# Moving the norm's reciprocal root behind the projections in a two-layer encoder

## The reference

```python
def _rms(x, g):
    y = x * rsqrt(mean(x * x, axis=-1) + EPS);  return y * g
# one layer
h = _rms(x, attn_norm);  z = h @ w_in            # 1024 -> 1984 columns
dq, dk = _rope(z[:, :512]), _rope(z[:, 512:1024])
dv, c_q, c_kv, k_pe = z[:, 1024:1536], z[:, 1536:1792], z[:, 1792:1920], z[:, 1920:]
y_diff = _rms(differential_attention(dq, dk, dv), diff_subln) * (1 - lam_init)
qh  = _rms(c_q, q_a_norm) @ w_q_b                # 4 heads of 128 + 64 (rope)
kvh = _rms(c_kv, kv_a_norm) @ w_kv_b             # 4 heads of 128 + 128
y_mla = latent_attention(qh, kvh, _rope(k_pe))
x = x + concat(y_diff, y_mla) @ w_o
h = _rms(x, ffn_norm)
x = x + (silu(h @ w_gate) * (h @ w_up)) @ w_down # 1024 -> 2816 -> 1024
```

## Time and profile before

| | |
|---|---|
| median of 3 runs | 2709.67 us |
| the profiled execution: its own time, its span | 2709.78 us, 2707.8 us |
| mean granted TensorE clock | 0.967 |
| TensorE busy | 2484.6 us (92%), 11236 matmuls |
| VectorE busy | 1328.9 us (49%) |
| ScalarE busy | 569.0 us (21%) |
| GpSimd busy | 892.0 us (33%) |
| the chain that ended last | TensorE 81%, VectorE 14%, issue 3%, ScalarE 1%, DMA 1% |

### The profile page before, as it was taken

One profiled execution on the slowest core, in us unless ns is written; L12 is line 12 of the kernel. 1 busy time (PEld: TensorE's weight loads), 2 busy tenths in 40 slices (PEclk: granted clock), 3 DMA queues, 4 the chain that ended last, 5 costly groups with the idle time before them and its releaser, 6 DMA issues.

```text
span 2707.8 us, 30377 instructions
## 1 busy us (share of the span) xinstructions
PE 2484.6 (92%) x11236; PEld 2024.4 (75%) x11236; DVE 1328.9 (49%) x2312; ACT 569.0 (21%) x1089; POOL 892.0 (33%) x434
## 2 busy tenths in 40 slices
PE   4888899896999999999989889988799999999996
PEld 3666687675888888888867668766578888888885
DVE  4887658857333223322248864886742222222225
ACT  2233314432010101010024341434111101000101
POOL 5431400014666655555210010001434433344421
PEclk9998999898999999999989999999899999999998
DMA  6431342122333333331122224222211111111101
GB/s 236 166 117 47 125 187 94 47 94 94 117 117 122 126 130 125 116 116 70 70 78 109 78 78 156 109 78 79 101 31 51 50 53 47 46 46 46 53 17 62
DMA packets 50339, 249.46 MB, mean 92 GB/s; under 512 B 5968, under 2 KB 6096, under 8 KB 32720
## 3 DMA queue, kind: packets, MB, share of 16 engines
q1 hardware_dynamic: 49824, 245.76, 25.5%
q10 hardware_dynamic: 432, 2.62, 0.2%
HBM read 187.54 MB, written 60.82 MB: 92 GB/s over the span
## 4 chain that ended last, share of the span: by engine, by line
PE 81%; DVE 14%; issue 3%; ACT 1%; DMA 1%; POOL 0%; SPq 0%; DVEq 0%; ACTq 0%; POOLq 0%
PE bank L412 26%; PE bank L413 25%; PE bank L414 25%; PE bank L747 1%; DVE acc L1129 1%; DVE mx L1263 1%; PE bank L614 1%; DVE qpe L1160 1%; DVE aT_lo L1271 1%; PE bank L621 1%; DVE h_lo L1116 1%; DVE h_t L1110 1%; ACT aT_hi L948 1%; DVE ms L1068 1%; DMA w<-parked 1%
## 5 line engine op out<-in xcount | busy, mean ns | idle before, releaser
L412 PE MATMUL bank<-h_hi,w 128*128 128x512 f32 x1792 | 708.8, 396 | 8.5 <-DVE h_lo L1116 6.2
L413 PE MATMUL bank<-h_lo,w 128*128 128x512 f32 x1792 | 701.5, 391 | 0.0
L414 PE MATMUL bank<-h_hi,w 128*128 128x512 f32 x1792 | 701.5, 391 | 0.0
L531 POOL TENSOR_TENSOR w<-raw,zero 128x1024 fp32r<-128x1024 f32 x159 | 314.0, 1975 | 951.7 <-PE bank L414 842.6
L1300 DVE TENSOR_TENSOR gated<-bank,silu 128x512 f32<-128x512 f32 x88 | 60.8, 691 | 749.8 <-PE bank L414 747.0
L412 PEld LDWEIGHTS bank<-h_hi,w 128*128 128x128 f32 x1792 | 339.5, 189 | 91.1 <-DVE h_lo L1116 13.4
L534 POOL TENSOR_TENSOR w<-raw,w 128x1024 fp32r<-128x1024 f32 x159 | 394.8, 2483 | 12.5
L413 PEld LDWEIGHTS bank<-h_lo,w 128*128 128x128 f32 x1792 | 339.3, 189 | 70.9 <-issue 1.7
L414 PEld LDWEIGHTS bank<-h_hi,w 128*128 128x128 f32 x1792 | 338.8, 189 | 71.6
L1310 DVE TENSOR_TENSOR x<-x,bank 128x512 f32<-128x512 f32 x352 | 238.4, 685 | 192.1 <-PE bank L414 191.8
L412 PE MATMUL bank<-u_hi,w 128*128 128x512 f32 x704 | 273.9, 389 | 0.0
(11 more groups left out here) (154 smaller groups left out, 3420.5 us busy)
## 6 DMA issues: line engine op xcount, KB each, us to landing
w<-parked SPq DMA_DIRECT2D x81, 1024.0 KB, 4.8
raw<-in_wffn SPq DMA_DIRECT2D x132, 512.0 KB, 3.6
parked<-w SPq DMA_DIRECT2D x27, 1024.0 KB, 4.8
parked<-p SPq DMA_DIRECT2D x27, 1024.0 KB, 4.9
raw<-in_watt SPq DMA_DIRECT2D x27, 512.0 KB, 5.7
praw<-in_watt SPq DMA_DIRECT2D x27, 512.0 KB, 5.8
out_yT<-y_out SPq DMA_DIRECT2D x16, 256.0 KB, 2.2
x<-in_xT SPq DMA_DIRECT2D x4, 512.0 KB, 5.7
```

Source lines behind the costliest of these rows:

```text
L412: nc.tensor.matmul(out_ap, lhs[0], rhs[0], start=first, stop=False)
L413: nc.tensor.matmul(out_ap, lhs[0], rhs[1], start=False, stop=False)
L414: return nc.tensor.matmul(out_ap, lhs[1], rhs[0], start=False, stop=last)
L531: nc.gpsimd.tensor_tensor(w[slot][0][:], src, zeros_like(src), ALU.add).then_inc(s_hi.sem, 1)
```

## The change

Projections now read x * gain, without the root; the root multiplies their results.

- **x_hi, x_lo**: ACT writes hi = x * gain (scale of the activation), DVE lo = x * gain - hi in one instruction with two SBUF inputs, as soon as a tile of x is there. h_t, AN and the applies are gone.
- **Where the root goes**: into the value projection's evictions (`scale=rstd`, one number per token and partition), into cos and sin tables for the rope tiles (`scaled`), into gate and up of the FFN (DVE multiplies the PSUM tiles in place), and for the latent tiles c_q and c_kv nowhere: their own norm follows, and only its EPS is scaled (`eps_var`).
- **first, next**: sums and spread of the norm are issued behind `values` and ahead of tile k0. ACT's v_hi waits for the root. At the seam of the layers x_lo follows each x add.
- **last**: sums come after both projections of ev 0, the spread after gate of ev 1; DVE adds a square and forms an x_lo in turn.
- **start**: DVE adds the first norm's squares in POOL's place; constants and rope tables are loaded from ACT's queue, x before and between the raw weights.
- **splits**: each of POOL's passes goes in two halves of 512 columns, and RAW is 2.
- **end**: the squares of batch 1 are added between the last x adds; both roots come before the 16 outputs.

```diff
-RAW = 3
+RAW = 2
 # POOL, split and prep
-                nc.gpsimd.tensor_tensor(w[slot][0][:], src, zeros_like(src), ALU.add).then_inc(s_hi.sem, 1)
+                for n, cols in enumerate(spans(2)):
+                    last = nc.gpsimd.tensor_tensor(w[slot][0][:, cols], src[:, cols], zeros_like(src[:, cols]), ALU.add)
+                last.then_inc(s_hi.sem, 1)
 # PE, FFN step 0
-                            if first and tt == 0:
-                                if b == 0:
-                                    pe.wait_ge(s_t_lo.sem, s_t_lo.half_at(l, 1, NSQ - 1))
-                                elif part == 0:
-                                    norm_spread("last", l)
...
-                            if first and ev == 0 and part == 0:
+                            if first and ev == 0 and part == 1:
                                 norm_sums("last", l)
+                            if first and ev == 1 and part == 0:
+                                norm_spread("last", l)
 # PE, halves
-            norm_sums("first", 0)
-            norm_spread("first", 0)
...
+                        if b == 0 and step == ("P", "k0"):
+                            norm_spread("first", l)
                         if kind == "V":
                             values(l, b)
+                            if b == 0:
+                                norm_sums("first", l)
 # ACT
+                nc.scalar.activation(hi[:, k, :], source(which, b, k), ACT.Copy, scale=gain_at(which, l, b, k)).then_inc(
+                    s_x_hi.sem, 1)
...
+                                act.wait_ge(s_dg.sem, s_dg.layer_at(l, 0))
...
-                                nc.scalar.activation(v[0][:, m, :], bank[2 + m][:], ACT.Copy).then_inc(s_plain_hi.sem, 1)
+                                nc.scalar.activation(v[0][:, m, :], bank[2 + m][:], ACT.Copy,
+                                                     scale=rstd[:, m:m + 1]).then_inc(s_plain_hi.sem, 1)
 # DVE
+                nc.vector.scalar_tensor_tensor(lo[:, k, :], source(which, b, k), gain_at(which, l, b, k),
+                                               hi[:, k, :].bitcast(F32), ALU.mult, ALU.subtract).then_inc(s_x_lo.sem, 1)
...
+            for k in range(KT):
+                x_lo("first", 0, 0, k)
+                square_add("first", 0, k)
...
+            def norm_use(which, l, b):
+                dve.wait_ge(s_rb.sem, f(s_rb, st0))
+                if which == "last" or which == "tail" and b == 1:
+                    nc.vector.tensor_copy(scaled[:, half, :], bank[tail][:]).then_inc(s_t.sem, 1)
                 else:
+                    nc.vector.tensor_tensor(scaled[:, 0, :], cs[:, 0, :], bank[tail][:], ALU.mult)
+                    nc.vector.tensor_tensor(scaled[:, 1, :], cs[:, 1, :], bank[tail][:], ALU.mult).then_inc(s_t.sem, 1)
...
                 for k in range(KT):
-                    last_add(l, k)
+                    square_add("last", l, k)
+                    x_lo("last", l, 0, k)
...
+                        nc.vector.tensor_tensor(zg[:], zg[:], scaled[:, b, :], ALU.mult).then_inc(s_gate.sem, 1)
+                        nc.vector.tensor_tensor(zu[:], zu[:], scaled[:, b, :], ALU.mult).then_inc(s_up.sem, 1)
...
+                        nc.vector.tensor_tensor(zu[:], zu[:], silu[ev % 2][:], ALU.mult).then_inc(s_gated.sem, 1)
```

More of the change, by code:

```diff
@@ L143 @@
 NSTAT_LAYER = B * NSTAT + 2
+USED = {}
+NORMED = {}
+for _s in STATS:
+    _n = 2 if _s == "cq" else 1
+    _at = sum(len(v) for v in USED.values())
+    USED[_s] = list(range(_at, _at + _n))
+    if _s != "n":
+        _at = sum(len(v) for v in NORMED.values())
+        NORMED[_s] = list(range(_at, _at + _n))
+NUSED = sum(len(v) for v in USED.values())
+NUSED_LAYER = B * NUSED + 2
+NNORMED = sum(len(v) for v in NORMED.values())
+NSPLIT_LAYER = (B + 2) * KT
 NEV = 2 * 16 + 16
@@ L1055, in _, with rsqrt_diagonal @@
             assert pre[0] == PRE_DVE
-            def rsqrt_diagonal(link, width, src, wait, done, dg=dg):
+            def rsqrt_diagonal(link, width, src, wait, done, dg=dg, eps=None, keep=False):
                 dve.wait_ge(*wait)
@@ L1311, in _, with down_add @@
-                link, n = chain(lambda j: s_link.layer_at(l, s_link.layer + j))
-                norm_rsqrt("next", l, 0, link)
+                def down_add(c, ev):
+                    dve.wait_ge(s_mm.sem, s_mm.step_at(l, c, 8 + ev))
+                    dve.wait_ge(s_xf.sem, s_xf.step_at(l, c, ev - 2 * KT))
+                    xn = x[:, ev // KT, ev % KT, :]
+                    nc.vector.tensor_tensor(xn, xn, bank[4 + ev % 4][:], ALU.add).then_inc(s_xf.sem, 1)
+                with dve.Fori(0, FC - 1) as c:
+                    gated_step(c)
+                    for ev in range(B * KT):
+                        down_add(c, ev)
@@ L1314, in _ @@
+                gated_step(FC - 1)
+                for ev in range(KT):
+                    down_add(FC - 1, ev)
+                link, n = chain(lambda j: s_link.layer_at(l, s_link.layer + j))
+                if l < L - 1:
+                    for k in range(KT):
+                        down_add(FC - 1, KT + k)
+                        x_lo("next", l, 0, k)
+                    norm_rsqrt("next", l, 0, link)
             n = [0]
@@ L1342, in _ @@
             assert n[0] == FINAL_DG
-            for m in range(4, B * KT):
-                if m == KT:
-                    dve.wait_ge(s_pe, 2)
+            dve.wait_ge(s_rb.sem, s_rb.layer_at(L, 0))
+            for m in range(KT):
+                output(m)
+            dve.wait_ge(s_pe, 2)
+            for m in range(KT, B * KT):
                 output(m)
```

366 lines of the change are left out of this document (197 added, 169 removed).

## The result

The changed kernel takes 2646.52 us (median of 4 runs, 2640.87 to 2648.54), the kernel before beside it 2709.5 (2706.43 to 2710.6): a ratio of 0.9759, 95% interval 0.9744 to 0.9773. The forecast was 2664, its range 2648 to 2692. The sign and most terms held, the size did not: 63 us were gained and 45.5 forecast. The profiled execution took 2646.8 us, span 2644.6, against 2709.8 and 2707.8.

What follows compares the result with a forecast made beforehand. TensorE, busy 2484.6 of 2707.8 us, was taken as the bound, so only its idle and slow-clock time could be won. The terms summed to -45.5 us from 2709.8, giving 2664 us, range 2648 to 2692.

Steps and rivals of the forecast that it cites:

- start: Head: the projection needs only x times gain, split in hi and lo, and starts at about 31 us; -8.6 us.
- first score, layer 0: Entry of layer 0's first half: with the root behind the values, the first score comes later; +3 us (0 to +7).
- first half, rest: Rest of layer 0's first half: less loss to waits behind held VectorE instructions and slow clock; -6 us (-14 to +2).
- FFN entries with the waits of 3.63: Tail of a half and FFN entry: that wait goes, second slot's gate starts earlier; -11 us per layer, -22 in all.
- layer 0 to 1, gap: Seam between the layers: the values begin at once after the FFN's last matmuls; -11.7 us.
- rivals 1: FFN entry and head mainly: port changes hands only between passes, so VectorE waits 2.6 us; 2688 us in all, chance 0.18.
- 3: First half and FFN entry: GpSimd's back-to-back instructions keep the port until its queue waits; +8, 2718 us, chance 0.05.
- Rival 4: Entries of the first halves: the late root lets VectorE's backlog grow; +8 us per entry, 2675 us, chance 0.12.
- Rival 2: Head, first half and FFN entries: holding of VectorE mostly vanishes; 2643 us in all, chance 0.10.
- held as now: Head, a bound: VectorE instructions held as long as in the kernel before; start at 36 us, 3 us gained.
- A chain of tiny links is held about as long as before: First half: chains of tiny VectorE instructions beside GpSimd's splits get no shorter with halves; no separate size.
- RAW 2 for 3: nothing: First half: with two raw buffers instead of three, loads still land in time; no effect on the time.

Runs made afterwards that it cites:

- experiment 4: The kernel before with GpSimd's passes in halves and two raw buffers instead of three; 2665.88 us, ratio 0.9828.
- kernel 2: The changed kernel with GpSimd's passes back at full width (1024 columns); 2658.45 us, ratio 0.9796.
- experiment 1: The kernel before with only GpSimd's passes cut in two halves of 512 columns; 2672.37 us, ratio 0.985.
- Experiments 5: The kernel before with 56 unused 128x512 matmuls in the wait at each FFN entry; 2703.99 us, ratio 0.998.
- 10: The changed kernel with attention sums inside the values, reordered head, and 46 unused matmuls in the wait for the FFN's sums; 2625.34 us, ratio 0.9684.
- Experiment 3: The kernel before with two raw weight buffers instead of three; 2700.98 us, ratio 0.9963.
- experiment 6: The changed kernel with the FFN's sums behind the second slot's gate and the spread behind its up; 2657.98 us, ratio 0.9807.
- kernels 8: The changed kernel with attention sums inside the values and the head reordered (setup, all lows of x, then adds); 2630.28 us, ratio 0.9706.
- 9: The changed kernel with attention sums inside the values, reordered head, and FFN sums behind the second slot's gate; 2642.47 us, ratio 0.9757.

## Why the prediction was right in sign and short in size

By its own steps, measured from the two profiles:

| step | forecast | measured |
|---|---|---|
| start | -8.6 | -9.0 |
| first score, layer 0 | +3 | +0.3 |
| first half, rest | -6 | -12.9 |
| FFN entries with the waits of 3.63 | -22 | -24.1 (-8.2, -8.6, -7.3) |
| second halves besides | 0 | -4.6 and -2.0 |
| layer 0 to 1, gap | -11.7 | -11.9 |
| first half of layer 1 | +0.1 (-2.5 + 2.6) | +2.7 |
| end | -1.3 | -1.8 |
| FFN loops; extras | 0; +1 | 0; in the stages |
| sum | -45.5 | -63.2 (of the spans) |

**Right:** the port's price. A held VectorE instruction takes 1.52 to 1.78 us (forecast 1.5), twelve of sixteen are held in the head, and the chains laid out from it came out within half a microsecond: first projection 30.67 for 31, the sums of the FFN 22.6 for 22.5 after its start, the second gate 24.3, first score of layer 1 at 18.63 for 18.9, values gapless in 21.8. By the trace, the port does pass between back-to-back GpSimd instructions without a semaphore between them, which the trace of before did not show; this settles against rivals 1 and 3. The Trainium skill ("SBUF — State Buffer", Who interferes with whom) has the lock held for one instruction, and the trace agrees: a held instruction waits for one half, not for the pass of two. Rival 4 (a growing backlog) is not seen in layer 1: the first score came on time and TensorE's idle time in that half fell from 23.3 to 21.7. In layer 0 the algebra did lengthen the half by 7.7 us (experiment 4), which is the rival's size, but only 0.6 of that is idle time. Rival 2's total of 2643 is near the result, but not its mechanism: nothing vanished, held instructions are as many as forecast (and its own terms add up to about 2640). A bound was wrong that cost nothing: "held as now" put the start at 36, and kernel 2, with full-width passes, starts at 30.93, since GpSimd's six instructions hold only six of VectorE's.

**Wrong:** the term "First half, rest". It was -6 and came to -12.9. The runs showed -14.9 for the halves alone and -5.4 for two raw buffers alone, adding up to -20.3, of which the algebra takes back 7.7 (forecast: the +3). With it failed two terms that stood at nothing: two raw buffers, and the second halves beyond their wait of 3.63 us (-4.6 and -2.0). The mechanism of the port was right, the sizes were not.

1. *The clock behind the waits had no price.* The prediction named "slow clock that follows" as part of the half's loss, and its -6 has no term for it. In experiment 1 the half gains 7.7 us of idle time and 7.3 of busy time. In all four profiles with full-width passes this half is busy for 265.2 to 267.4 us, in all eight with halves for 256.1 to 264.4. Experiments 5 and 10 show the clock's price by itself, 3.1 us for a wait of 13.7, 2.2 and 3.0 for one of 11.4. Over the whole kernel idle time fell by 46.5 us, close to the 45.5 forecast, and busy time by 16.7, for which the forecast had hardly more than the 2.5 of layer 1's values. That the first two numbers are so close is partly luck, since single terms are off both ways.
2. *"A chain of tiny links is held about as long as before"* was right: the chains beside splits take 10.4 and 7.5 us with halves, 10.1 and 5.0 without. What the -6 undersold are the large held instructions on the way to a product: the waits for kd_lo, behind those of the rope, alone fell by 6.4 us in experiment 1.
3. *"RAW 2 for 3: nothing"* was wrong even by its own numbers, since a pair of chunks was to take 12.05 us against TensorE's 10.9. Above all it asked only whether a load would be late, and not what a late load leaves free: in the pause the root's chain slips through. Experiment 3 shows this mechanism as a gain, experiment 6 its reverse.
4. The second halves were not priced beyond the wait. Halves alone shorten them by 5.9 and 4.5 us (experiment 1; 2.5 and 4.5 in experiment 4), but the changed kernel with full-width passes has them as short as any (268.8 and 271.5, experiment 2). So either edit gets most of it. How it splits into waiting and clock is not steady: in the changed kernel idle time fell by 3.4 us and busy time by 4.9 in layer 0, in layer 1 idle time fell by 6.2 and busy time rose by 0.6. What in the algebra shortens them no run shows.

At the FFN entries the forecast had nearly the right sum by a reason that is only half right: halves alone gained 6.7 each (experiment 1), the algebra with full-width passes 7.9 and 8.1 (69.0 and 69.1 in kernel 3, 61.1 and 61.0 in kernel 2), and both together 8.2 and 8.6. Either of them removes nearly the same wait, so the gains of the two don't add there, while in the first half halves and raw buffers do.

**Open:** why the algebra lengthens the first half by 7.7 us. Only 0.6 of that is idle time (38.0 to 38.6), 7.1 is busy time (256.1 to 263.2), and about 2 of these are the sums and the spread, which stood ahead of the half before. Behind the small change of idle time stand larger ones: the waits for dg rose from 9.6 to 13.2 us, the last root's chain from 6.8 to 9.7, so the gain of two raw buffers is lost there again, and other waits fell. The rest is clock, and part of it may be chance: the six kernels with algebra and halves are busy for 260.3 to 264.4 in this half. The first half of layer 1 came out 2.7 longer (272.0 to 274.7). The late-sums kernel has the same code there and took 272.5, kernels 8, 9 and 10, alike among themselves, 273.3, 272.3 and 270.0, so this much comes without any cause in the code.

## What to carry to other kernels

Price a wait of TensorE with what follows it: here each long wait cost another 2 to 3 us at the lower clock, and half of what shorter waits gave back in the first half was clock.

Where two engines share a port, look for the held instructions that the critical engine waits for. Cutting GpSimd's passes in two, which takes more of GpSimd's time (130.4 us instead of 117.0 in the first half), let large instructions of VectorE through sooner and was worth 37 us alone. It did nothing for a chain of tiny ones. For such a chain it counts where GpSimd's long work lies: a later load moved it away and gave 8 us, and work put into the wait that sheltered the chain moved it there, in a kernel that lost 11.

What an edit is worth depends on what stands beside it: the halves gave 37 us in the kernel before and 12 in the changed one. So take a change of several edits apart from both ends even when it wins; one of its parts may be losing in a stage (the algebra in the first half) and another winning unseen (the raw buffers).

## What the runs showed of the hardware

- Back-to-back GpSimd instructions with no semaphore between them let a waiting VectorE instruction in at each boundary, and GpSimd's own then take longer: the two at 622.54 took 3.26 us between them, two of the same kind alone take 2.54. Holding goes both ways.
- A 128x512 instruction of VectorE with two SBUF inputs took 2.4 to 2.8 us beside GpSimd's passes of 1024 columns and 1.52 to 1.78 beside passes of 512. A chain of 12 tiny ones (128x4) did not gain: 10.1 and 10.4 us, 5.0 and 7.5; undisturbed it takes 3.1.
- With matmuls whose results nobody uses in the wait, the granted clock stayed up: 46 of 128x512, 10.6 us of a wait of 11.4, and it was 1.00 through the entry, where it had been 0.89.
